# A decoder step on one core: each 1 MB weight block requested as two transfers of 512 KB

## What is computed

```python
proj = x @ w_in                       # 7184 columns: ua, va, q, k, v, r, gk_low, g_a, g_b
y_a = chunk_spatial_gate(gelu(ua), layernorm(gelu(va)), w_s, b_s)
y_b = silu(r) * rmsnorm(gla(q, k, v, log_a, S0))            # gated linear attention, 4 heads
m = sigmoid(g_a) * (y_a @ w_br_a) + sigmoid(g_b) * (y_b @ w_br_b)
x1 = layernorm(alpha * x + m @ w_o)
# PEER: 8 heads; top 16 of 128 x 128 experts by product keys of the query x1 @ w_q
h = gelu(einsum('thkd,td->thk', u_tab[idx], x1))
peer = einsum('thk,thkd->td', gate * h, v_tab[idx])
x2 = layernorm(alpha * x1 + peer)
x3 = x2 + (p @ w_pe) * sigmoid(x2 @ w_pg)
```

## Time and profile before

| | |
|---|---|
| time, median of 3 runs | 1989.66 us (1983.47 to 1993.34) |
| the profiled execution's own time | 1995.63 us |
| its span | 1993.5 us |
| mean granted TensorE clock | 0.822 |
| PE busy | 1443.4 us (72%) |
| DVE busy | 1164.6 us (58%) |
| POOL busy | 990.9 us (50%) |
| DMA, moved | 675.81 MB, mean 339 GB/s |
| queue q0 (gathers) | 545.33 MB, 69.9% of 16 engines |
| queue q1 (SP) | 129.23 MB, 17.4% of 16 engines |
| DMA packets | 188404, of which under 8 KB 174482 |

### The profile page before, as it was taken

How to read it: one execution, slowest core, us unless ns; L and a number is a source line. 1 busy time by engine, 2 the same in 40 slices (tenths; PEclk the granted TensorE clock), 3 DMA queues, 4 the chain that set the end, 5 groups by cost and what they waited for, 6 DMA issues and landing times.

```text
span 1993.5 us, 19824 instructions
## 1 busy us (share of the span) xinstructions
PE 1443.4 (72%) x6736; PEld 906.0 (45%) x6736; DVE 1164.6 (58%) x2987; ACT 406.0 (20%) x813; POOL 990.9 (50%) x1052
## 2 busy tenths in 40 slices
PE   9999996689888779889886788246542436674546
PEld 7888885576554347556653455013220101131113
DVE  1110112776777657685667755687678877866511
ACT  2310200224232222131111212121122211121000
POOL 0000000336665556665555655677666677767760
PEclk9999998799997779998898899667676665687588
DMA  6344442689999999999999899999999999999992
GB/s 255 119 146 148 148 149 85 251 305 412 410 411 412 389 377 405 410 412 412 408 407 377 327 380 374 399 406 398 405 379 364 374 409 409 409 396 399 409 387 87
DMA packets 188404, 675.81 MB, mean 339 GB/s; under 512 B 36329, under 2 KB 38505, under 8 KB 174482
## 3 DMA queue, kind: packets, MB, share of 16 engines
q0 software_dynamic: 149760, 545.33, 69.9%
q1 hardware_dynamic: 38546, 129.23, 17.4%
HBM read 667.07 MB, written 7.41 MB: 338 GB/s over the span
## 4 chain that ended last, share of the span: by engine, by line
PE 43%; DMA 25%; DVE 16%; POOL 7%; issue 5%; ACT 2%; SPq 1%; DVEq 0%; PEldq 0%; POOLq 0%
PE PJ L1383 13%; DMA at<-in_v_tab,idxV 13%; PE PJ L1281 10%; PE Y L1433 7%; DVE at L1164 6%; DMA at<-in_u_tab,idx 5%; PE PJ L1288 4%; POOL at L637 4%; POOL at L646 3%; PE PJ L1267 3%; DMA at<-in_w_q 2%; DMA at<-in_p_t 1%; DMA at<-in_state 1%; PE PJ L1342 1%; DMA out_st_s<-at 1%
## 5 line engine op out<-in xcount | busy, mean ns | idle before, releaser
L637 POOL DMA_INDIRECT at<-in_u_tab,idx x512 | 486.8, 951 | 642.3 <-DVEq L1147 351.5
L1164 DVE CUSTOM_DVE_ANT_0 at<-at,XD 128x1024 f32<-128x1024 f32 x512 | 614.6, 1216 | 200.4 <-DMA at<-in_u_tab,idx 187.5
L646 POOL DMA_INDIRECT at<-in_v_tab,idxV x512 | 487.2, 952 | 319.4 <-PE Y L1433 181.4
L1433 PE MATMUL Y<-at,at 128*32 128x512 f32 x2048 | 344.3, 792 | 317.5 <-DMA at<-in_v_tab,idxV 306.5
L1383 PE MATMUL PJ<-at,at 128*128 128x256 f32 (+1 forms) x1792 | 416.5, 392 | 2.1 <-issue 1.1
L1383 PEld LDWEIGHTS PJ<-at,at 128*128 128x128 f32 x1792 | 345.0, 195 | 78.1 <-issue 19.4
L1433 PEld LDWEIGHTS Y<-at,at 128*32 128x32 f32 x2048 | 73.4, 130 | 504.1 <-issue 488.8
L1281 PE MATMUL PJ<-at,at 128*128 128x256 f32 (+2 forms) x960 | 240.5, 412 | 41.8 <-DMA at<-in_w_q 28.5
L1281 PEld LDWEIGHTS PJ<-at,at 128*128 128x128 f32 (+2 forms) x960 | 179.0, 190 | 104.0 <-DMA at<-in_w_q 31.2
L1267 PE MATMUL PJ<-at,at 128*128 128x256 f32 (+1 forms) x640 | 143.6, 383 | 0.0
L1267 PEld LDWEIGHTS PJ<-at,at 128*128 128x128 f32 (+1 forms) x640 | 107.6, 171 | 38.6 <-issue 12.6
(11 more groups left out here) (208 smaller groups left out, 1333.4 us busy)
## 6 DMA issues: line engine op xcount, KB each, us to landing
at<-in_w_blk SPq DMA_DIRECT2D x72, 1024.0 KB, 7.9
at<-in_w_q SPq DMA_DIRECT2D x16, 1024.0 KB, 8.7
at<-in_w_o SPq DMA_DIRECT2D x8, 1024.0 KB, 6.5
at<-in_u_tab,idx POOLq DMA_INDIRECT x512, 11.8
at<-in_v_tab,idxV POOLq DMA_INDIRECT x512, 11.1
at<-in_state SPq DMA_DIRECT2D x4, 1024.0 KB, 8.2
out_st_s<-at SPq DMA_DIRECT2D x4, 1024.0 KB, 7.1
at<-in_w_pg SPq DMA_DIRECT2D x2, 2048.0 KB, 13.2
```

Source lines behind the costliest of these rows:

```text
L637: pool.indirect_dma_start(ubuf[slot], None, u_tab, bass.IndirectOffsetOnAxis(rows_of, 0)).then_inc(u_in[slot], 16)
L646: pool.indirect_dma_start(vbuf[slot], None, v_tab, bass.IndirectOffsetOnAxis(rows_of, 0)).then_inc(v_in[slot], 16)
L1164: v.tensor_tensor_reduce(out=t, in0=t, in1=XD[:, :], scale=1.0, scalar=0.0, op0=ALU.mult, op1=ALU.add, accum_out=hraw[:, n % 2, k:k + 1]). ...
L1433: last = mm(Y[32 * c:32 * c + 32, s, :], wpadV[d // PAIR % 2][:, g, :], vbuf[slot][:, 512 * s:512 * s + 512], start=False, stop=final)
```

## The change

`load_block` issues two transfers for every block instead of one. Each carries half of the chunks (4 of 8 for w_blk, 2 of 4 for w_o and w_q) for all 128 partitions, so that a partition's part of a transfer is 4 KB instead of 8 KB. Both raise the same semaphore by 16, and `block_of` waits for 32 per use of the buffer instead of 16. The bytes, the layout in SBUF and HBM, the order of the blocks and the waits on SP are the same.

```diff
                 if s >= RING:
                     sp.wait_ge(pj_done, last_job(STREAM[s - RING]) + 1)
-                if b[1] == "wo":
-                    sp.dma_start(ring_wide[s % RING], w_o[b[2]][:, 4 * b[3]:4 * b[3] + 4, :]).then_inc(blk_in[s % RING], 16)
-                elif b[1] == "wq":
-                    sp.dma_start(ring_wide[s % RING], w_q[b[2]][:, 4 * b[3]:4 * b[3] + 4, :]).then_inc(blk_in[s % RING], 16)
-                else:
-                    sp.dma_start(ring[s % RING], w_blk[BLOCKS.index(f"{b[1]}{b[2]}")]).then_inc(blk_in[s % RING], 16)
+                for half in range(2):
+                    if b[1] in ("wo", "wq"):
+                        chunks = slice(4 * b[3] + 2 * half, 4 * b[3] + 2 * half + 2)
+                        src, dst = (w_o if b[1] == "wo" else w_q)[b[2]][:, chunks, :], ring_wide[s % RING][:, 2 * half:2 * half + 2, :]
+                    else:
+                        chunks = slice(4 * half, 4 * half + 4)
+                        src, dst = w_blk[BLOCKS.index(f"{b[1]}{b[2]}")][:, chunks, :], ring[s % RING][:, chunks, :]
+                    sp.dma_start(dst, src).then_inc(blk_in[s % RING], 16)
...
                 s = AT[b]
-                pe.wait_ge(blk_in[s % RING], 16 * (s // RING + 1))
+                pe.wait_ge(blk_in[s % RING], 32 * (s // RING + 1))
                 return s % RING
```

## The result

The change makes the kernel slower: median 2003.94 us (1996.13 to 2011.02, 20 runs) against 1990.97 us (1983.47 to 1998.0, 20 runs). The ratio is 1.0066, with a 95% interval of 1.0053 to 1.0079, so 10.6 to 15.7 us, about 13. The forecast was 1997.0 with 1986 to 2006: the direction and the range hold, the size was nearer twice the 7.2 us of the sum.

The account below looks back on a forecast made before the run. DMA was taken as the bound from 440 to 1080 us, with TensorE's stalls for weight blocks mattering elsewhere. Bytes 3.2, early stalls 2.2 and late stalls 1.8 sum to 7.2 us on the 1989.66 median: 1997 us, range 1986 to 2006.

Parts of the forecast that it names:

- Issues: SP's queue: one more DMA instruction for each of 96 blocks, covered by the first half's transfer; 0, at most 1 us.
- Latency of its own: Each half's fixed transfer latency: halves queued behind each other add only their bytes, so 0.
- Smaller packets: Blocks requested from 440 to 1080 us, where DMA bounds: 0.08 us more for each of 40, 3.2 us (0 to 5.2).
- Shares: Stalls for w_o and w_q: queues alternate by packet, so blocks beside gathers drop from two thirds to half; +1.5 us each.
- What reaches the end: Of the eight stalls' growth: early four paid in full, 2.2 us; 1038 us stall 0; last three 0.6 us each, 1.8.
- all stalls at full price: Rival: stalls, state loads and upper byte cost all paid in full; 17.9 us, 2007.6 us; chance 0.16.
- the states': Three state exchanges: a block in 4 KB packets ahead in the same queue delays each state load by 1.5 us.
- the dearer bytes: Extra DMA engine time for blocks in 4 KB packets where DMA is full, taken at its upper 5.2 us.
- Only the bytes: Rival: every stall made up by gathers running ahead, or early ones hidden; 0 to 3.2 us, 1991.5 us; chance 0.27.
- gathers gain: Rival: from 440 to 1080 us gathers move more beside blocks, so row waits shrink; -9 us, 1981 us; chance 0.07.
- latency twice: Rival: each half pays 2.5 us fixed latency in turn at eight stalls; 23 us, 2013 us; chance 0.05.

Follow-up runs that it names:

- the changed kernel again: The changed kernel, unaltered, run and profiled once more on another chip as a yardstick: ratio 1.0049 (1.0026 to 1.0071) to the kernel before.
- the kernel with the tiny transfer: The kernel before with its one transfer of 8 KB runs per block, plus a second transfer of 2 KB that TensorE also waits for: ratio 0.9996 (0.9972 to 1.0019).

## Why the prediction was right and wrong, point by point

*Issues: 0, cover about 1.2 us.* Right for the time (0.9996 with a second transfer for every block). Not right in detail: SP needed 2.68 us for the four issues at 395 us where four of 0.4 us would be 1.6. The row is SP's timeline of the changed kernel:

```profile
395.09 2.68 SPq L510 DMA_DIRECT2D at<-in_w_q  x4
```

*Latency of its own: 0.* Right where nothing else is in the queues: at 307 us 4.73 us from the second request, 5.1 from the first, and 5.04 before. In the stalls of 393 to 421 us three of four profiles with a second transfer are longer, but slow issues are not shown to be how: with only w_o and w_q split the four issues took 2.08 us and the stall was 5.7 us, and in the changed kernel again 1.76 us and 9.0 us (each from the second request). The estimate from the Trainium skill, DMA: Bandwidth & Descriptors, its rules for kernel authors (1 MiB per DMA) and its anatomy of one DMA (a fixed 2.0 us for each), was 16 us for the eight stalls. The kernel with the tiny transfer disagrees with its 0.9996, and the one with a single transfer of 4 KB runs lost time with transfers of 1 MB. What the rule advises was right for this kernel, for another reason.

*Smaller packets: 3.2 us (0 to 5.2).* Wrong, what reached the time was its lower end. Split w_blk blocks alone gave 0.9988 (0.9965 to 1.0010, which still allows 2 us), and the lateness was 6.0 us ahead of the full stretch and 5.9 behind it. The DMA share there is 1.02 as before, but the table of stretches shows TensorE busy for 546 of the 640 us (547 before):

```profile
440.00:1080.00 640.00, 546.34 (x2663) 353.06 (x2665) 433.56 (x1110) 158.28 (x315) 370.56 (x391) 0.91 1.02 403
```

That the share reads full was taken as "any DMA time more is time more". The engines did spend more on the split blocks in this pair of profiles. From 60 to 280 us, where blocks go alone, the queue of the blocks reads, before and changed:

```profile
q1 hardware_dynamic: 5258, 30.79, 41.1%
```

```profile
q1 hardware_dynamic: 9122, 30.52, 42.3%
```

That is 3.8% more engine time for each MB, or 0.1 us of a block's 2.5, and yet no time was lost by it. How much of it is real is open: the five profiles with w_blk in two transfers of 4 KB runs read 0.1 to 3.8% more for each MB than the kernel before, the two with one transfer of 4 KB runs 0.3% more and 1.2% less.

*Shares: +1.5 us in five stalls, +0.3 in two, 0.1 in one.* The mechanism is shown: two thirds, a half and three eighths of the bytes with runs of 8, 4 and 2 KB, at nearly equal packet counts (whether the engines change queue after each packet or after several is not shown). From the release of the buffer, the last stall is 8.5, 9.5 to 9.9 and 12.7 us long (without the kernel with the tiny transfer), and the w_o stall at about 1050 us 8.4 to 8.7, 9.9 to 10.2 and 12.5 us. That is 1.0 to 1.8 us more with 4 KB, where 1.5 was forecast. The four late stalls of the changed kernel grew by 1.5, -0.5, 1.6 and 1.4 us. At 375 us the 1.5 us did not come (6.7 us after, 6.6 before; 6.9 to 7.2 in the other profiles with 4 KB). At 394 and 416 us 0.3 each was forecast, and it was 3.4 and 1.3. For the one at 394 us the prediction used a row of the other; its own window, shown above, has 0.59 MB of gathers beside 1.29 MB of the block in the kernel before, so gathers were not absent there. The sum over all eight, 8.2 us, was close to the 8.9 us by which the stalls grew, but by errors that offset each other in the early ones.

*What reaches the end: 4.0 of these 8.2 us.* This is the step that failed. The w_o stall was set at 0 because DMA is full around it, and the three behind it at 0.6 instead of 1.5 because the gathers would run ahead. The runs show that longer stalls reach the end in full, within their errors: 10.5 us more of waits and 13 us more of time; with 2 KB, 54.5 us of waits against 39.3 of the kernel with only w_blk split, 15 us more, and 0.89%, which is 18 us of time (12 to 25). The stall at 1038 us, priced at 0, grew by 1.5 us, and the changed kernel is later by at least that at the next stall: its w_q row starts 8.2 us late where the w_o row had started 5.9 us late. A single profile has errors of a few us, so this is one for one within that, and not the half that was forecast. Part of it is not the stalls' own length but the clock behind them, 2.8 us, which the prediction did not consider. No gain from gathers that run ahead can be seen; why, no run here shows. The chain has no gather between the late stalls, and between the last three nothing but TensorE, which is the nearest that the profile says.

So of 13 us the prediction had 7.2, of which 3.2 were not there; that the range held was in part luck, since two errors of opposite sign went into the sum. The rival *all stalls at full price* had the right step (full passage) and two wrong terms, the states' and the dearer bytes; 17.9 us was as far on the other side. *Only the bytes* is refuted by the two kernels that split some of the blocks (0.9988 and 1.0050), *gathers gain* by the sign, *latency twice* by the kernel with the tiny transfer.

## What to carry to other kernels

When two queues share the DMA engines, look at the packet sizes of both before cutting a transfer up: here each queue got about as many packets as the other, so the one with shorter runs got fewer bytes, and the bytes that an engine stood and waited for came later. Cost such a change at the stalls of the engine that waits, even where DMA reads full: made longer, the stalls on the chain reached the end in full here, and taken away they gave back two thirds. Count every stall from the release of the buffer: the rows of split transfers start later. Look at the clock of the matmuls behind a stall as well. And here removing the stalls was worth more than any setting of the transfer that ends them: cutting the blocks so that none was requested and needed at once gave 1.2 to 1.3%, which no choice of run length came near.

## What the runs showed of the hardware that was not expected

A transfer of 64 partitions ran at half rate. In the kernel split by partitions, blocks alone in the queues (314 to 318 us; packets, MB, share):

```profile
q1 hardware_dynamic: 142, 0.90, 102.4%
```

0.90 MB in 4 us is 0.23 MB per us with the engines busy throughout, where transfers of 128 partitions moved 0.42. The stall there was 6.91 us from its second request, against 5.04 from the only one. The Trainium skill, DMA: Bandwidth & Descriptors, rules for kernel authors, calls two transfers to disjoint partition halves not worth while because both use the same engines; the share of 102.4% of 16 engines agrees. Its section on the descriptor swizzle puts the partitions 0 to 63 behind half of SBUF's ports, which might give half the rate; no run here tells whether it does.
